# Four re-orderings in a one-core fp32 encoder layer: attention bias by rounded products, merged columns, router, last expert

## The reference, cut to what matters

```python
h = rmsnorm(x, g_mix); proj = h @ w_in            # q, k, v, pool, z, xbc, dt, three gates
s = q @ k.T + rel_table[rel_bucket(kpos - qpos)]  # 4 heads x 2 maps, chunk-causal mask
attn = softmax(s0) - lam * softmax(s1)            # differential attention
merged = g0 * (attn_out @ w_b0) + g1 * (pool_out @ w_b1) + g2 * (ssd_out @ w_b2)
x = x + merged @ w_mix_out
x = x + cross_attention(rmsnorm(x), rmsnorm(mem))
# 16 experts in 4 groups: top-1 group, top-2 experts in it
x = x + sum(comb[:, e] * ((silu(h @ w_gate[e]) * (h @ w_up[e])) @ w_down[e]))
return rmsnorm(x, g_final)
```

## Time and profile before

| | |
|---|---|
| three runs | 513.97, 513.95, 514.27 us (median 513.97) |
| the profiled execution | 513.97 us, span 512.2 us |
| busy: PE, PEld, DVE, ACT, POOL | 492.1, 333.9, 247.9, 195.6, 15.7 us |
| DMA | 149.28 MB, mean 291 GB/s |
| TensorE clock, mean of the span | 0.992 of full |

### The profile page before, as it was taken

The page is one execution under the profiler, slowest core; times in us unless marked ns, Lnnn a source line. Parts: engine busy times, 40 slices in busy tenths (PEclk is TensorE's granted clock), DMA queues, the critical chain, the costliest instruction groups (busy, mean ns, idle before and its releaser), DMA issues.

```text
span 512.2 us, 7124 instructions
## 1 busy us (share of the span) xinstructions
PE 492.1 (96%) x2772; PEld 333.9 (65%) x2772; DVE 247.9 (48%) x469; ACT 195.6 (38%) x349; POOL 15.7 (3%) x30
## 2 busy tenths in 40 slices
PE   7999999999999999999999899999999999999982
PEld 7998998778888988788998534433443344433330
DVE  3764599876788689985664621111111111111113
ACT  5454757446726455445674201111211121111113
POOL 2000100000030000000100000000000000000000
PEclk9999999999999999999999899999999999999998
DMA  7797647643544548896769999999999999999992
GB/s 252 260 312 200 216 132 226 194 117 119 160 162 153 197 125 279 277 355 199 268 230 371 405 401 394 400 399 402 404 402 399 401 400 404 404 399 399 400 357 87
DMA packets 68026, 149.28 MB, mean 291 GB/s; under 512 B 8790, under 2 KB 15124, under 8 KB 67988
## 3 DMA queue, kind: packets, MB, share of 16 engines
q1 hardware_dynamic: 67684, 148.24, 80.5%
q10 hardware_dynamic: 304, 0.53, 0.3%
HBM read 147.69 MB, written 1.05 MB: 290 GB/s over the span
## 4 chain that ended last, share of the span: by engine, by line
issue 47%; PE 34%; DVE 14%; ACT 2%; DMA 1%; POOL 0%; SPq 0%; POOLq 0%; DVEq 0%; ACTq 0%
PE bank L1422 9%; PE bank L1424 9%; PE bank L1423 9%; DVE wl L930 6%; DMA raw<-in_w_in 1%; DVE gates L1189 1%; DVE xc L946 1%; ACT wh L570 1%; PE bank L1445 1%; PE bank L1532 1%; DVE gates L1192 1%; PE bank L1555 1%; DVE big L976 1%; DVE al L916 1%; DVE al L923 1%
## 5 line engine op out<-in xcount | busy, mean ns | idle before, releaser
L930 DVE TENSOR_TENSOR wl<-raw,wh 128x1024 fp32r<-128x1024 f32 (+1 forms) x80 | 94.2, 1195 | 35.2 <-ACT wh L570 33.7
L570 ACT ACTIVATE wh<-raw 128x1024 fp32r<-128x1024 f32 (+1 forms) x80 | 81.9, 1043 | 67.5 <-PE bank L1424 50.8
L1422 PE MATMUL bank<-wh,ah 128*128 128x512 f32 (+2 forms) x248 | 95.0, 383 | 0.0
L1423 PE MATMUL bank<-wl,ah 128*128 128x512 f32 (+2 forms) x248 | 93.3, 376 | 0.0
L1424 PE MATMUL bank<-wh,al 128*128 128x512 f32 (+2 forms) x248 | 93.3, 376 | 0.0
L1424 PEld LDWEIGHTS bank<-wh,al 128*128 128x128 f32 x248 | 46.6, 188 | 8.6
L1422 PEld LDWEIGHTS bank<-wh,ah 128*128 128x128 f32 x248 | 46.7, 188 | 8.3 <-issue 0.3
L1423 PEld LDWEIGHTS bank<-wl,ah 128*128 128x128 f32 x248 | 46.7, 188 | 7.8
L1422 PE MATMUL bank<-ah,wh 128*128 128x256 f32 x160 | 45.8, 286 | 2.2 <-DVE al L916 1.2
L1423 PE MATMUL bank<-al,wh 128*128 128x256 f32 x160 | 45.3, 283 | 0.0
L1424 PE MATMUL bank<-ah,wl 128*128 128x256 f32 x160 | 45.2, 283 | 0.0
(11 more groups left out here) (352 smaller groups left out, 900.1 us busy)
## 6 DMA issues: line engine op xcount, KB each, us to landing
raw<-in_w_in SPq DMA_DIRECT2D x48, 512.0 KB, 4.7
wh_raw<-in_w_exp_up SPq DMA_DIRECT2D x14, 512.0 KB, 12.4
wl_raw<-in_w_exp_gate SPq DMA_DIRECT2D x13, 512.0 KB, 11.2
gates<-in_w_exp_down SPq DMA_DIRECT2D x13, 512.0 KB, 13.3
raw<-in_w_branch SPq DMA_DIRECT2D x12, 512.0 KB, 4.1
ah_raw<-in_w_exp_up SPq DMA_DIRECT2D x10, 512.0 KB, 12.2
al_raw<-in_w_exp_gate SPq DMA_DIRECT2D x10, 512.0 KB, 11.4
gates<-in_w_exp_gate SPq DMA_DIRECT2D x9, 512.0 KB, 11.5
```

Of the source, the lines that this page charges most:

```text
L570: act.activation(dst, src, ACT.Copy, scale=scale).then_inc(done, 1)
L930: dve.tensor_tensor(wl[:, n % RING, 0:sz], raw[:, n % RING, 0:sz], wh[:, n % RING, 0:sz].bitcast(F32), ALU.subtract)\
L1422: pe.matmul(dst, st[0], mv[0], start=start, stop=False, skip_group_check=True)
L1423: pe.matmul(dst, st[0], mv[1], start=False, stop=False, skip_group_check=True)
```

## The change

1. **Bias.** ScalarE copies `flip` into a rounded `flip_r` and the table into `bias_hi`, 256 and 128 columns of each of four heads, in iteration 13. VectorE writes `bias_lo` in iteration 14. `scores` turns each part with one 384-column fp32r product. GpSimd fills the table's masked corner before the memory norms rather than after.
2. **Order.** In a slot `scores(s)` is issued ahead of `attn_T(s-1)`.
3. **Merge.** The transposes of the merged halves are issued after chunks 63 and 65 instead of 62 and 64.
4. **Router.** Eleven filler products stand ahead of the ranks; the second row tile's first rest part is made after `select(0)`; the first gather takes both hi parts before the lo parts.
5. **Last expert.** `down`, `y_hi`, `y_lo` and `scatter` of expert 15's second unit are cut into two halves of 256 columns, in banks 0 and 3.
6. **Mean square.** ScalarE scales by D^-0.5 inside the square, so that VectorE needs one operation instead of two.

```diff
-WARM = (10, 6, 5, 6, 0, 0, 4, 3)
+WARM = (10, 6, 5, 6, 0, 0, 4, 11)
...
             for t in range(T):
                 norm_rstd("h", t, rs, ss)
+            g.wait_ge(s_("toep_in"), 16 * HEADS)
+            g.memset(toep[64:P, :, S - SEEN:S], LOW).then_inc(s_("toep_ready"), 1)
...
+                if n == FIRST["bcd"] + 1:
+                    act.wait_ge(s_("consts_set"), 1)
+                    act.activation(flip_r[:, :], flip[:, :], ACT.Copy).then_inc(s_("toep_ready"), 1)
+                    act.wait_ge(s_("toep_ready"), 2)
+                    hi_of(bias_hi[:, :, 0:256], toep[:, :, :], s_("toep_ready"))
+                    hi_of(bias_hi[:, :, 256:384], toep[:, :, P:S], s_("toep_ready"))
...
-                link(dve.tensor_tensor(ss, ss4[:, 0:2], ss4[:, 2:4], ALU.add))
-                dve.tensor_scalar(ss, ss, 1.0 / D, EPS, ALU.mult, ALU.add).then_inc(s_("x_mean_square"), 1)
+                dve.scalar_tensor_tensor(out=ss, in0=ss4[:, 0:2], scalar=EPS, in1=ss4[:, 2:4], op0=ALU.add, op1=ALU.add)\
+                    .then_inc(s_("x_mean_square"), 1)
...
+                if n == FIRST["bcd"] + 2:
+                    dve.wait_ge(s_("toep_ready"), 4)
+                    for at, lo in ((0, 0), (256, P)):
+                        dve.tensor_tensor(bias_lo[:, :, at:at + S - lo], toep[:, :, lo:S], bias_hi[:, :, at:at + S - lo].bitcast(F32),
+                                          ALU.subtract).then_inc(s_("toep_ready"), 1)
...
-            for t in range(T):
-                moe_rows(t, 0, D // 2)
-
+            moe_rows(0, 0, D // 2)
...
             select(0)
+            moe_rows(1, 0, D // 2)
...
-                for t, w, lo, _, d in blocks:
-                    mm = pe.matmul(d, flip[:, :], toep[:, h, lo:lo + w], start=False, stop=True, skip_group_check=True)
+                for dst in (pS1, pS0):
+                    for part in (bias_hi, bias_lo):
+                        mm = pe.matmul(dst[:, 0:384], flip_r[:, :], part[:, h, :], start=False, stop=part is bias_lo, skip_group_check=True)
...
+                if 0 <= s < 4:
+                    scores(s)
                 if 1 <= s < 5:
                     attn_T(s - 1)
-                if 0 <= s < 4:
-                    scores(s)
...
-                if n in (FIRST["b21"], LAST["mka"]):
-                    half = int(n == LAST["mka"])
+                if n in (LAST["b21"], FIRST["m0"]):
+                    half = int(n == FIRST["m0"])
...
+            keep_warm(WARM[7], bank[2])
...
+            def down_last(j, fill):
...
+                for c, dst in zip(COL_HALF, y_last_bank):
+                    for kk in range(2):
+                        kt = 2 * j + kk
+                        for i in range(2):
+                            mm = pe.matmul(dst[row_half[i], 0:256], aT[:, kt, row_half[i]], w[i][:, kk, c], start=(kt == 0), stop=(kt == 3),
+                                           skip_group_check=True)
+                    if j and c is COL_HALF[0]:
+                        mm.then_inc(filled, 1)
+                mm.then_inc(spent, 1)
```

More of the change, by code:

```diff
@@ L1380, in _ @@
                     cols_out(g + 1, 2 * (e - 2) + 1, bank[3], 4 * (g + 1) + 2 * (e - 2) + 2)
-                if n >= 2:
-                    last = n == EXPERTS + 1
-                    y_lo(yl_last if last else yl, yh_last if last else yh, p, ybank(n - 2), n - 1)
+                if 2 <= n <= EXPERTS:
+                    y_lo(yl[:, :], yh[:, :], p, bank[1][:, :], n - 1)
+                if n == EXPERTS + 1:
+                    for j, c in enumerate(COL_HALF):
+                        y_lo(yl_last[:, c], yh_last[:, c], p, y_last_bank[j][:, 0:256], EXPERTS + j)
             with dve.If(over > 0):
@@ L1397, in _ @@
                             for half in range(2):
-                                y_lo(yl, yh, p, bank[1], r * EXPERTS + EXPERTS + 2 * p + half + 1)
+                                y_lo(yl[:, :], yh[:, :], p, bank[1][:, :], r * EXPERTS + EXPERTS + 2 * p + half + 2)
             def gained(half, t):
@@ L1830, in fill_of, with scatter_last, first_gather @@
                 return fast_fill(UNIT[kind, n, j])
-            pe.wait_ge(s_("sel_ready"), 1)
-            pe.wait_ge(s_("moe_rows"), T)
-            gather(0, 0, bank[3])
+            def down_last(j, fill):
+                slot, times = fill
+                pe.wait_ge(arrived_x[slot], times * 32)
+                w = [HOMES[2 * slot + i][0].rearrange("p (k n) -> p k n", k=2) for i in range(2)]
+                for c, dst in zip(COL_HALF, y_last_bank):
[7 more added lines that the diff above has]
+                mm.then_inc(spent, 1)
+            def scatter_last():
+                for j, c in enumerate(COL_HALF):
+                    pe.wait_ge(s_("y_lo"), EXPERTS + j)
+                    for t in range(T):
+                        for part in (yh_last, yl_last):
+                            mm = pe.matmul(bank[5 + 2 * t][:, c], selT[:, 1, t, :], part[:, c], start=False, stop=True, skip_group_check=True)
+                        if j:
+                            mm.then_inc(s_("scatter_pe"), 1)
+            def first_gather():
+                pe.wait_ge(s_("sel_ready"), 1)
+                pe.wait_ge(s_("rows_hi"), T)
+                for rows in (rows_hi, rows_lo):
+                    if rows is rows_lo:
+                        pe.wait_ge(s_("moe_rows"), T)
+                    for t in range(T):
+                        for kt in range(2):
+                            mm = pe.matmul(bank[3][:, 256 * kt:256 * kt + 256], rows[:, t, 0:256].rearrange("a (p k) -> a k p", k=2)[:, kt, :],
+                                           sel[:, 0, t, :], start=(rows is rows_hi and t == 0 and kt == 0), stop=(rows is rows_lo and t == T - 1),
+                                           skip_group_check=True)
+                mm.then_inc(s_("gather_pe"), 1)
+            first_gather()
             gather(0, 1, bank[2])
```

66 lines of the change are left out of this document (39 added, 27 removed).

## The result

The changed kernel took **515.56 us** in the median of 20 runs (513.51 to 521.2), the kernel before 514.21 us in 20 runs beside it (513.49 to 515.75): ratio 1.0044, interval 1.0028 to 1.0061, so it is slower by 0.4%. The medians differ by 0.3%, the ratio by more, because the times of the changed kernel have a long upper tail: twelve runs lie at 513.5 to 515.9 and show a mean TensorE clock of 0.990 or more; eight stretch from 516.8 to 521.2, and seven of these show 0.988 or 0.987. The profiled execution is one of the seven: 520.22 us, span 518.5, clock 0.987.

What follows compares the result with a forecast made beforehand. VectorE sets the pace in 60.5 to 99 us, TensorE from about 131 to 280, full DMA engines from 266.30 nearly to the last unit. +1.42 (delay until the merge's end) - 1.02 (tail) = +0.4 on 513.97: 514.4 us, range 511.5 to 516.0.

Steps and rivals of the forecast that it cites:

- The added split: Bias parts on ScalarE and VectorE: chunk 18's split 2.8 us late, bounds 1.8 to 3.4.
- Nothing takes it up: Front, chunk 18 to 21: the 2.8 us delay passes on whole; TensorE idles about 3 us ahead of chunk 21.
- Attention: Four heads: VectorE's rounds set their end; TensorE leaves 1.37 us late, the delay minus 1.38.
- Merge: Merged halves' transposes: the 0.82 us wait moves ahead of chunk 65; edit costs 0.05, other end -0.82.
- The tail: Last unit to mean square: halves and fused mean square save 1.0 us, bounds -0.4 and -1.3.
- rival 3: Last unit: half passes are load-bound, rows at 0.3 instead of 0.21 us a pass; 514.9 us, chance 0.05.
- The router: Ahead of the ranks: fillers delay them about 1 us, taken as zero because the full DMA queue covers it.
- rival 1: Front: the added split is mostly hidden, delay near 0 to 1 us; 511.6 to 512.6 us, chance 0.22.
- Rival 4: Tail's gain is real and the merge gains its 0.82 us; 513.5 us, chance 0.10.
- The slower one I had: TensorE's 3 us stand ahead of chunk 21 drops its clock; 515.9 us for 7 us at half clock, chance 0.13.
- My list of signs of being wrong: Chunk 21 on time, clock under 1 in 71-90 us, or last unit moved by something besides SyncE's restart.

Runs made afterwards that it cites:

- after: The profiled execution of the changed kernel in its first measurement: 520.22 us, span 518.5 us.
- a1: The changed kernel unchanged, timed and profiled again: 518.7 us, ratio 1.0084 to the kernel before.
- b4: a8 plus the bias parts, ScalarE's ahead of its dt wait, VectorE's subtractions behind the split of chunk 19: 511.76 us, ratio 0.9945.
- a6: The kernel before with the bias parts, turned products and scores ahead of the transposes: 514.91 us, ratio 1.0003.
- a7: The kernel before with only each head's scores ahead of the previous head's transposes: 513.49 us, ratio 0.9980.
- a3: The changed kernel without the 22 filler passes, rest parts and first gather as changed: 515.3 us, ratio 1.0019.
- a2: The changed kernel with its three router edits undone (fillers, rest-part order, split first gather): 515.05 us, ratio 1.0009.
- before: The profiled execution of the kernel before the change: 513.97 us.
- a4: The kernel before with the three router edits alone: 516.7 us, ratio 1.0045.
- b1: The kernel before with the 22 filler passes alone: 516.21 us, ratio 1.0032.
- b3: The kernel before with 44 filler passes instead of 22: 517.65 us, ratio 1.0067.
- b2: The kernel before with the new order of the rest parts and the split first gather, no fillers: 514.84 us, ratio 1.0015.
- a8: The kernel before with scores ahead of the transposes and the changed tail (a7 and a5 together): 513.23 us, ratio 0.9974.
- a5: The kernel before with only the tail changed (last down product in column halves, fused mean square): 513.79 us, ratio 0.9986.

## Why the prediction was wrong

It said no change: +0.4 us, 514.4, with a range of 511.5 to 516.0. The kernel is slower by 0.4%, or 1.4 to 3.1 us by the interval, which is more than the 1.0 us that I called no change. The step that failed is the one on the router, whose delay was put at nothing because the DMA queue is full; the runs show a queue that covers 1.3 us of delay, and fillers, rest parts and half clock that together took up to 4.5. That the median, 515.56, lies in the range is luck: the range's upper end came from a fall of the clock at chunk 21, which did not happen.

**The added split: right ahead of the waits, 0.5 too dear behind them.** Chunk 18's split came 2.71 us late against 2.78 forecast (7.08 behind chunk 15's instead of 4.37). "Nothing takes it up" failed in part: at chunk 19 it was 2.43, at chunk 20 2.33, at chunk 21 2.28. 0.26 of the 0.43 that went on the way was taken up where ScalarE's split of chunk 19 follows the dt exponential (0.13 us behind its start, 0.39 before). TensorE's wait ahead of chunk 21 was 2.49 us against "about 3". From chunk 15's split to SyncE's restart the front as a whole lost 1.0 us in after and 0.9 in a1, against 1.42 forecast. b4 shows that the rest is a matter of place: the same work costs nothing 4 us further on. The chain of waits had 1.56 us of ScalarE's and 2.67 us of VectorE's idle time in it, usable by anything that stands behind the chain's own work.

**Attention: right, the sum and its parts.** The forecast was 1.38 us back between chunk 21 and the transposes of head 3; it was 1.47 there (60.24 us behind chunk 21 instead of 61.71), and 1.39 at the restart (a6). The forecast had two parts, and so has the trace. VectorE's last mix was to come 0.72 nearer to chunk 21, by the earlier scores; it came 0.81 nearer, in a7, a6 and after alike (59.83 instead of 60.64). The transposes were to follow the mix's end by 0.06 us instead of 0.72; they follow by 0.06 in after and 0.05 in a6, but still by 0.68 in a7. So this second part belongs to the cheaper turned products, which the prediction left without a cause: with the old flips TensorE itself is late there, with the new ones it waits for VectorE (0.26 us, 129.84). At the restart the two parts are 0.86 and 0.53.

**Merge: right.** The wait of 0.82 us is gone, one of 1.11 (forecast 0.85) stands ahead of chunk 65, and the edit costs 0.04 to 0.12 us (restart behind chunk 21 196.80, 196.81, 196.83 and 196.88 in a1, a3, a2 and after, 196.76 in a6 and 196.70 in b4, without the edit) against 0.05, or up to 0.18 by b4.

**The tail: right.** -0.84 against -1.0. The half passes follow each other at 0.21 to 0.22 us with loads of 0.14 us beside them, so rival 3 did not happen. By the Trainium skill (TensorE: Matmul & The Clock Gate, Part 3, "What overlaps and what doesn't"), which lets weight loads overlap running matmuls only when their row groups differ, the prediction's estimate put half a microsecond there; these rows speak against it, for passes of this width too.

**The router: the step that failed.** The prediction's words were "Taken as zero: the full DMA queue is the cover. If it ran dry there, each us would count in full." The queue was full at 401 GB/s, but I never measured how much it held. SyncE's unit into x waits for the last rest part of the rows (which ends at 288.14 in before and 292.79 in after, 0.08 and 0.07 us ahead of the issue), and the ledger shows what such a delay may cost: about 1.3 us beyond the 21.9 of before is free (a6), 2.0 us is not (a3). Three things used it up:
- The rest parts behind the ranks: the last ends 3.0 us behind the key instead of 2.3, +0.7. I had not followed this edit to SyncE's wait.
- The fillers: forecast about 1 us of delay. It was 2.1 us in a1, a4 and b1 and 2.5 between a3 and after.
- The clock. I said the fillers "keep the clock that stood at 0.50", and set the gain of that against their delay. In eight profiles it fell at 279 to 281 us, while TensorE ran the router's passes of 20 columns or the first residual passes behind them, ahead of the place where the fillers stand. In after it was back at full speed at 286.4, when the first filler ran (286.30), and in a3 at 286.2 with no filler at all: they bought nothing. Worse, the half clock stretches the residual passes ahead of them (six passes 2.82 us in before, 4.52 in a1, 5.47 in after). In after VectorE has the choice of experts ready at 285.1 (L1324), the fillers start at 286.30, and so lie wholly in the path of the ranks. With no half clock (b3) some 2 us of them are free. None of the five profiles with fillers shows the late fall (283 to 285.5 us) that before, b2 and b4 show; but in before and b4 that fall costs the unit into x nothing (21.92, 21.93).

In after the sum is 1.3 (key late by the half clock alone, a6) + 2.5 + 0.7 = 4.5 us, the 4.46 by which the distance grew (26.38 - 21.92).

**Each us beyond the cover counted for more than one.** From 24.06 to 26.38 us U grows by 3.9, not 2.3. The units behind the one into x wait for the first expert's passes, which start late too: in 294 to 300 us the share was still 0.77, and SyncE issued into zs 3.1 us later than before (295.09, 291.95). It is one execution at 26.38; between 24.06 and 24.81 us four profiles lie from 235.07 to 236.16, in no clear order.

**The rivals.** Of rival 1 only 0.5 us came true. Rival 4 did not: the merge's wait moved. Rival 3's 514.9 rests on the estimate of 0.5 us; by rows at 0.3 us a pass it would have been 515.0. The slower one I had was a clock fall behind the stand at chunk 21; the granted clock stayed at 1.00 in 60 to 99 us of after. The clock had a part, but in the router: 1.3 of the 4.5 us, and it set how much of the fillers lay in the path. My list of signs of being wrong did name it: the last unit's start moved by something other than SyncE's restart.

**What stays open.** What makes the clock fall at 279 us in one execution and at 285 or not at all in another isn't settled: the router's instructions up to there are the same in all of these kernels but for the mean square, TensorE stood idle for 1.3 us ahead of the ranks in a7, a8, b4, b2 and before alike and only three of them lost the clock behind it, and nothing tried here controls it. That the longer runs of the changed kernel are those with the long half clock rests on the listed clocks (seven runs at 0.987 or 0.988 took 516.8 to 521.2 us, one at 0.992 took 519.9) and two profiles, not on a run in which the clock was forced. a1 doesn't bear it out: its six runs show 0.988 to 0.992, and the longest, 519.59 us, has 0.992. So that link is argued and not shown. Why all six runs of a1 were above 517 is open too; the three series ran on three chips and that of the first measurement isn't on record, so a difference between chips is a rival that nothing here tests. a2's ratio (+0.5 us, 0.0 to 0.9) leaves some 0.4 us beyond the sum of its parts (front +0.95, tail -0.84).

## What to carry to other kernels

A full queue is a cover of a certain depth, not a cover: find the transfer whose issue waits for the work you delay, and read how long the queue lasts behind it, before you price a delay at nothing. Work that is added to a chain of short waits cost nearly its whole length ahead of them here (2.3 of 2.7 us) and nothing in their idle time, so try the idle time that the profile shows before you give the edit up. Filler work behind the place where the clock falls is only work; whether it would hold the clock if it stood ahead of that place was not tried.

## What was not expected of the hardware

- The half clock stood in the router in 11 of 14 profiles, at a place that moved from 279 to 285.5 us, and lasted between 3 and 7 us; a7, a8 and b3 had none. Just before it fell in after the profile shows TensorE busy all the time (277.5 to 279: 1.50 of 1.50 us), with passes of 20 columns.
- The first microseconds differ by 0.6 us between two executions of the changed kernel (chunk 15's split at 47.65 in after, 48.27 in a1) and by 1.1 us over the 14 profiles, and the last stretch behind VectorE's scaling by 1.6 us (5.6 to 7.2). Distances between two events inside the trace repeat to 0.1 us where no edit lies between them (198.14, 198.15, 198.13 us from chunk 21 to the restart in a5, before and b1), so they show edits that the medians of 12 runs can't.
